# A hybrid decoder trunk: every fourth weight block's low half subtracted by GpSimd in the projection, output and query stages

## The reference

```
h = rmsnorm(x, norm1_g[l]) * (1 + sc1) + sh1
x = x + g1 * token_mixer(h, positions, w_in[l], ret_gn_g[l], sinks[l], w_out[l])
h = rmsnorm(x, norm2_g[l]) * (1 + sc2) + sh2
x = x + g2 * peer(h, peer_wq[l], k1[l], k2[l], peer_u[l], peer_v[l])
```

## Time and profile before

| | |
|---|---|
| time, median of 3 runs | 1949.06 us (1948.62 to 1949.06) |
| span of the profiled execution | 1948.0 us |
| PE busy | 1901.1 us (98%) |
| DVE busy | 1725.7 us (89%) |
| ACT busy | 1201.8 us (62%) |
| POOL busy | 575.5 us (30%) |
| `w_lo` subtractions on DVE | 664, 814.3 us, 1227 ns each |

### The profile page before, as it was taken

The page is one execution under the profiler, slowest core; times in us unless marked ns, Lnnn a source line. Parts: engine busy times, 40 slices in busy tenths (PEclk is TensorE's granted clock), DMA queues, the critical chain, the costliest instruction groups (busy, mean ns, idle before and its releaser), DMA issues.

```text
span 1948.0 us, 37761 instructions
## 1 busy us (share of the span) xinstructions
PE 1901.1 (98%) x13826; PEld 1830.6 (94%) x13826; DVE 1725.7 (89%) x3225; ACT 1201.8 (62%) x2215; POOL 575.5 (30%) x404
## 2 busy tenths in 40 slices
PE   6999999999999999999999999999999999999998
PEld 6899899999999999999978898999999999999998
DVE  7788888999799899999988978899988888999997
ACT  4478545666788645555456775466667885555554
POOL 0000000000799544555200000000019873455550
PEclk8999999999999999999999999999999999999999
DMA  9776765666565799999867756656664558999994
GB/s 338 248 254 217 261 226 176 204 204 204 203 199 191 247 377 375 370 379 373 309 225 261 251 169 221 223 187 202 205 206 164 173 173 306 373 373 366 367 381 163
DMA packets 139940, 503.72 MB, mean 259 GB/s; under 512 B 16632, under 2 KB 17272, under 8 KB 139304
## 3 DMA queue, kind: packets, MB, share of 16 engines
q1 hardware_dynamic: 115048, 411.95, 61.0%
q0 software_dynamic: 24768, 90.19, 11.8%
HBM read 496.69 MB, written 1.57 MB: 256 GB/s over the span
## 4 chain that ended last, share of the span: by engine, by line
PE 72%; DVE 20%; issue 3%; ACT 2%; DMA 2%; POOL 1%; SPq 0%; DVEq 0%; ACTq 0%
PE ps L1893 19%; PE ps L1889 12%; DVE w_lo L919 7%; PE ps L1574 7%; PE ps L1493 6%; PE ps L1489 5%; PE ps L1490 4%; PE ps L1578 4%; PE ps L1486 3%; PE ps L1849 2%; PE ps L1620 1%; DVE hot L1232 1%; DVE hot L1224 1%; ACT w_hi L596 1%; PE ps L1776 1%
## 5 line engine op out<-in xcount | busy, mean ns | idle before, releaser
L596 ACT CAST w_hi<-raw 128x1024 fp32r<-128x1024 f32 x664 | 697.1, 1050 | 687.7 <-PE ps L1889 264.4
L919 DVE TENSOR_TENSOR w_lo<-raw,w_hi 128x1024 fp32r<-128x1024 f32 x664 | 814.3, 1227 | 145.6 <-ACT w_hi L596 141.2
L571 POOL TENSOR_SCALAR hot<-con,rt 128x128 f32<-128x128 f32 x216 | 268.7, 1255 | 545.7 <-DVE neg L1404 517.0
L1574 PE MATMUL ps<-h_both,w_hi 128*128 128x432 f32 x1712 | 373.2, 359 | 0.0
L1574 PEld LDWEIGHTS ps<-h_both,w_hi 128*128 128x128 f32 x1712 | 305.6, 189 | 10.0
L1489 PE MATMUL ps<-h_both,w_hi 128*128 128x256 f32 (+1 forms) x920 | 224.3, 284 | 2.8 <-ACT big L876 2.2
L1578 PEld LDWEIGHTS ps<-h_both,w_lo 128*128 128x128 f32 x1712 | 223.4, 191 | 2.8 <-DVE w_lo L919 0.6
L1578 PE MATMUL ps<-h_both,w_lo 128*128 128x216 f32 x1712 | 224.0, 273 | 0.0
L1490 PE MATMUL ps<-h_both,w_hi 128*128 128x256 f32 (+1 forms) x920 | 220.3, 280 | 0.0
L1893 PE MATMUL ps<-p_both,w_hi 128*128 128x432 f32 x992 | 214.9, 358 | 1.4 <-DVE p_both L1329 1.4
L1893 PE MATMUL ps<-h_both,w_hi 128*128 128x432 f32 x960 | 207.8, 358 | 0.1
(11 more groups left out here) (234 smaller groups left out, 2862.2 us busy)
## 6 DMA issues: line engine op xcount, KB each, us to landing
raw<-in_u SPq DMA_DIRECT2D x256, 512.0 KB, 3.3
raw<-in_v SPq DMA_DIRECT2D x256, 512.0 KB, 6.1
raw<-in_win SPq DMA_DIRECT2D x104, 512.0 KB, 4.4
hot<-in_ada SPq DMA_DIRECT2D x62, 512.0 KB, 4.8
big<-in_ada SPq DMA_DIRECT2D x34, 512.0 KB, 6.5
raw<-in_wq SPq DMA_DIRECT2D x32, 512.0 KB, 4.6
raw<-in_wout SPq DMA_DIRECT2D x16, 512.0 KB, 4.2
big<-in_decay SPq DMA_DIRECT2D x2, 1536.0 KB, 7.9
```

Of the source, the lines that this page charges most:

```text
L571: last = nc.gpsimd.tensor_scalar(hot2[:, b % 2, t, :], iota, rt[:, 1, col], rt[:, 2, col], ALU.is_equal, ALU.mult)
L596: nc.scalar.copy(w_hi[:, j % 2, :], raw[:, j, :]).then_inc(hi_ready, 1)
L919: tt(w_lo[:, j % 2, :], raw[:, j, :], w_hi[:, j % 2, :].bitcast(F32), ALU.subtract).then_inc(lo_ready, 1)
L1574: mm(o[:, 0:2 * DENSE].rearrange("p (a t) -> p a t", a=2), w_hi[:, s, P * k:P * (k + 1)], h_both[:, :, k, 0:DENSE], start=(k == 0), stop=F ...
```

## The change

GpSimd makes the low half of some blocks, VectorE that of the others. A new table says which:

```diff
+MIX_LOWS = range(11, B_WOUT + 4), range(3, B_WOUT + 4)
+LOW_POOL = tuple(tuple(m for m in range(3, N_BLOCKS, RING) if m in MIX_LOWS[l] or B_WQ < m < B_U) for l in range(DEPTH))
+def by_pool(n):
+    return n % N_BLOCKS in LOW_POOL[n // N_BLOCKS]
+def low_count(n):
+    return sum(by_pool(k) == by_pool(n) for k in range(n + 1))
...
             def low(n, j):
+                if by_pool(n):
+                    return
                 dve.wait_ge(hi_ready, n + 1)
```

With `B_WOUT` = 52, `B_WQ` = 60, `B_U` = 76 and `RING` = 4 these are blocks 11, 15, ..., 55 of layer 0 (12 blocks), 3, 7, ..., 55 of layer 1 (14), and 63, 67, 71, 75 of either (8): 34 of 664. No block of `u` or `v` is among them. GpSimd runs, ahead of its additions of squares and behind them:

```diff
+            def low(n):
+                pool.wait_ge(hi_ready, n + 1)
+                nc.gpsimd.tensor_tensor(w_lo[:, n % 2, :], raw[:, n % RING, :], w_hi[:, n % 2, :].bitcast(F32), ALU.subtract
+                                        ).then_inc(lo_pool, 1)
...
+                lows(l, 0, B_WQ)
                 pair_squares(2 * l + 1)
+                lows(l, B_WQ, B_V)
```

Low halves are now counted by two semaphores, `lo_ready` (VectorE) and the new `lo_pool` (GpSimd). Whoever waits for one low half waits for the semaphore of its maker:

```diff
+                if n >= RING:
+                    sp.wait_ge(low_sem(n - RING), low_count(n - RING))
...
-                pe.wait_ge(lo_ready, n + 1)
+                pe.wait_ge(low_sem(n), low_count(n))
```

More of the change, by code:

```diff
@@ L341, in build @@
         raw_in = [sem(f"raw_in{s}") for s in range(RING)]
+        lo_pool = sem("lo_pool")
         hi_ready, lo_ready, block_done, out_taken = map(sem, ("hi_ready", "lo_ready", "block_done", "out_taken"))
@@ L396, in home, with low_sem @@
             return (M if m < 2 or C_AQ <= m < C_AQ + 2 else E)[m % 2]
+        def low_sem(n):
+            return lo_pool if by_pool(n) else lo_ready
         block = ctx.enter_context(nc.Block())
@@ L403, in load, with loads_between @@
                 n = base + RING * i + j
-                ge(sp, lo_ready, n - RING + 1)
+                if n >= RING:
+                    sp.wait_ge(low_sem(n - RING), low_count(n - RING))
                 sp.dma_start(raw[:, j, :], src(l, RING * i + j)).then_inc(raw_in[j], 16)
+            def loads_between(src, first, end, base, l):
+                per = [sum(by_pool(base + RING * (first - 1) + k) == by_pool(base + RING * (first - 1) + j) for k in range(RING))
+                       for j in range(RING)]
+                with sp.Fori(first, end) as i:
+                    for j in range(RING):
+                        n = base + RING * (first - 1) + j
+                        sp.wait_ge(low_sem(n), low_count(n) + per[j] * (i - first))
+                        sp.dma_start(raw[:, j, :], src(l, RING * i + j)).then_inc(raw_in[j], 16)
             ada_all = ada.rearrange("l n p d -> (l n) p d")
@@ L522, in _ @@
                     if q == 3:
-                        with sp.Fori(first, SPREAD_AT) as i:
+                        for i in (0, 1):
                             for j in range(RING):
                                 load(src, i, j, base, l)
+                        loads_between(src, 2, SPREAD_AT - 1, base, l)
+                        for j in range(RING):
+                            load(src, SPREAD_AT - 1, j, base, l)
                         sp.wait_ge(tok_copied, 2 * (l + 1))
@@ L537, in _ @@
                         first = N_U // RING
[L538 to L541, removed]
+                    assert first == count // RING
                     if q == 1:
@@ L557, in pair_squares, with lows @@
                     nc.gpsimd.tensor_tensor(sq[:, k, :], sq[:, k, :], sq[:, k + 1, :], ALU.add).then_inc(sq_paired, 1)
+            def low(n):
+                pool.wait_ge(hi_ready, n + 1)
+                nc.gpsimd.tensor_tensor(w_lo[:, n % 2, :], raw[:, n % RING, :], w_hi[:, n % 2, :].bitcast(F32), ALU.subtract
+                                        ).then_inc(lo_pool, 1)
+            def lows(l, first, end):
+                for m in LOW_POOL[l]:
+                    if first <= m < end:
+                        low(l * N_BLOCKS + m)
             for l in range(DEPTH):
@@ L577, in _ @@
                 pool.wait_ge(gate_mat, N_GATE * (l + 1))
+                used_at = [dot_at(k) for k in range(SP_STEPS)] + [mix_at(k) for k in range(SP_STEPS)]
+                low_next = B_V
                 for j in range(2 * SP_STEPS):
+                    if j >= SP_SLOTS:
+                        upto = B_V + used_at[j - SP_SLOTS] + 3
+                        lows(l, low_next, upto)
+                        low_next = max(low_next, upto)
                     if j >= SP_SLOTS:
@@ L585, in _ @@
                         bass.IndirectOffsetOnAxis(spread[:, 0, k:k + 1].bitcast(U32), 0)).then_inc(row_in[slot], 16)
+                lows(l, low_next, N_BLOCKS)
             pair_squares(2 * DEPTH)
@@ L1557, in project_pair @@
                 with_lo(0, KC - 1).then_inc(block_done, 1)
-                pe.wait_ge(lo_ready, n + 2)
+                pe.wait_ge(low_sem(n + 1), low_count(n + 1))
                 for k in range(KC):
@@ L1565, in add_half, with project_wide @@
                           skip_group_check=True)
-            def project_wide(l, m, j, after_wide=True, first=FIRST_U[0], halves=0):
+            def project_wide(l, m, j, after_wide=True, first=FIRST_U[0], halves=0, turn=0):
                 s, n = j % 2, l * N_BLOCKS + B_U + m
+                at = l * N_BLOCKS + B_U + j
                 pe.wait_ge(hi_ready, n + 1)
@@ L1575, in project_wide @@
                        start=(k == 0), stop=False, skip_group_check=True)
-                pe.wait_ge(lo_ready, n + 1)
+                per = sum(by_pool(at + k) == by_pool(at) for k in range(LONG))
+                pe.wait_ge(low_sem(at), low_count(at) + per * turn)
                 for k in range(KC):
@@ L1894, in both_y, with outputs_y, low_wait @@
                               (h_both[:, :, j - 2, 0:nd] if j >= 2 else p_both[:, j, :, 0:nd]), start=begin, stop=False, skip_group_check=True)
-                def outputs_y(i, blocks, first=False, last_ones=False):
+                def outputs_y(i, blocks, first=False, last_ones=False, turn=0):
+                    def low_wait(j):
+                        at = l * N_BLOCKS + B_V + RING * i + j
+                        per = 0
+                        if not isinstance(i, int):
+                            at = l * N_BLOCKS + B_V + RING + j
+                            per = sum(by_pool(at + k) == by_pool(at) for k in range(RING))
+                        pe.wait_ge(low_sem(at), low_count(at) + per * turn)
                     for j in range(blocks):
@@ L1908, in outputs_y @@
                                 if which == 2:
-                                    pe.wait_ge(lo_ready, n + 1)
+                                    low_wait(j)
                                 for c in range(KC):
@@ L1935, in _ @@
                 with pe.Fori(1, SP_SUM_AT // RING) as i:
-                    outputs_y(i, RING)
+                    outputs_y(i, RING, turn=i - 1)
                 sum_mixed()
```

2 lines of the change are left out of this document (1 added, 1 removed).

## The result

The changed kernel takes 1966.25 us (median of 4 runs, 1962.43 to 1966.97) against 1949.06 us: a ratio of 1.0082, 95% interval [1.0068, 1.0097]. By the medians it is 17.2 us slower. The forecast was 7.5 us slower, with a range that ended at 1964.0: the sign was right, the size was not.

What follows compares the result with a forecast made beforehand. The prediction took TensorE to set the pace. Its terms, 1.7 + 2.3 + 1.5 + 1.1 + 0.9 = 7.5 us, on the 1948.0 us span plus 1.06 us gave 1956.6 us, range 1945.5 to 1964 us.

Steps and rivals of the forecast that it cites:

- What bounds the kernel: TensorE sets the pace; VectorE costs time only where TensorE waits for it, 4.8 us in layer 0.
- Cost of one moved block: Projection, output and query stages: frees 1.14 us on VectorE, takes 2.45 us on GpSimd; the engines exclude each other.
- The four places: Tight stretches in projection and output stages of both layers: +1.7, +2.3, +1.5 and +1.1 us.
- blocks 11 to 16: Layer 0: block 11 gets 0.7 us faster, later rotations and angle instructions come late; +1.7 us.
- layer 0's output stage: Blocks 51 and 55 each delay VectorE by 1.15 us, and block 60's load hangs behind; +2.3 us.
- The other 26 moved blocks: Elsewhere, mostly free as TensorE doesn't wait for `w_lo` or VectorE reads PSUM; +0.9 us for all.
- Bookkeeping, query stages: Waits, queue order and `u` and `v` register sums cost nothing new; GpSimd isn't still at work ahead of query blocks.
- The sign of being wrong: VectorE subtractions all staying at 1.22 us, or a falling total of `w_lo` waits, would make the prediction wrong.
- rival (1): GpSimd leaves the port between its pieces and VectorE passes, so waits vanish; about 1944.5 us, chance 0.15.
- (2): Collisions fall mostly into VectorE's idle time, gains and losses cancel within 3 us; 1946 to 1952.5 us, chance 0.25.
- (3): Behind gapless VectorE work moved blocks take 4 to 5 us, 15 of 34 hold TensorE up; about 1966 us, chance 0.12.

Runs made afterwards that it cites:

- Relief alone: Changed kernel without GpSimd's 34 subtractions, nobody making these low halves, so its result is wrong; 1947.89 us, -1.9 us against the kernel before.
- the kernel with the ends: Changed kernel with only 16 projection and output stage blocks moved to GpSimd; 1956.63 us, +6.4 us against the kernel before.
- the ten attention blocks alone: Changed kernel with only blocks 27, 31, 35, 39 and 43 of each layer on GpSimd; 1958.44 us, +8.0 us against the kernel before.
- the kernel with the empty table: Changed kernel with no block moved, VectorE making all 664 low halves and the bookkeeping kept; 1950.86 us, ratio 1.000 against the kernel before.
- pieces: Changed kernel with each moved GpSimd subtraction cut into four of 256 columns; 1969.89 us, +17.9 us against the kernel before.
- A GpSimd copy with one input: VectorE makes every low half; GpSimd runs copies of 1024 columns into an idle buffer at 26 points; 1955.16 us, +4.9 us against the kernel before.
- the subtraction over 512: VectorE makes every low half; GpSimd runs 26 dummy subtractions over 512 columns; 1955.44 us, +5.7 us against the kernel before.
- two blocks: Changed kernel with only block 39 of layer 0 and block 27 of layer 1 on GpSimd; 1956.03 us, +6.6 us against the kernel before.
- the long dummy: VectorE makes every low half; GpSimd runs 26 dummy subtractions over 1024 columns into an idle buffer; 1965.26 us, +14.4 us against the kernel before.
- the eight: Changed kernel with only attention blocks 27, 31, 35, 43 of layer 0 and 31, 35, 39, 43 of layer 1 moved; 1953.01 us, +3.1 us.

## Why the prediction was wrong, point by point

- **What bounds the kernel**: held. Relief alone is worth 2 us, less than the 4.8 us of waits that the forecast read in layer 0.
- **Cost of one moved block**: held. 2.38 us against 2.45; full exclusion; VectorE stands still for up to 2.2 us (two-column addition: 0.16 to 2.36 us), 1.5 us on average, for 1.14 us freed. The Trainium skill (SBUF — State Buffer, "SBUF: two separate sides") calls the shared pair "an exclusive lock, not a bandwidth split", held for the whole instruction, against VectorE instructions with two SBUF inputs or in a two-port mode. The trace agrees for the lock (four masked maxima that read PSUM, beside GpSimd's 2.39 us from 147.38, take their usual 0.48 us; the first of them is shown):

```profile
147.38 2.39 POOL L591 TENSOR_TENSOR w_lo<-raw,w_hi 128x1024 fp32r<-128x1024 f32 x1 [14.03 <-ACT w_hi L646]
147.70 0.48 DVE L1142 CUSTOM_DVE_ANT_0 big<-ps,big,vec 128x256 f32<-128x256 f32 x1 [0.72 <-PE ps L1763]
```

- **The four places** (forecast 6.6 us): 7.15 us by the shifts, 6.4 us by the kernel with the ends. The working of single places was rougher than the sum. In blocks 11 to 16, block 11 went as written (the second rotation stood until 63.1), but at block 15 what stood still was a cast ahead of the angle instructions, which the forecast had not named:

```profile
73.42 3.12 POOL L591 TENSOR_TENSOR w_lo<-raw,w_hi 128x1024 fp32r<-128x1024 f32 x1 [10.90 <-ACT w_hi L646]
74.22 2.47 DVE L994 CAST iota<-con 128x256 f16<-128x256 f32 x1
```

  In layer 0's output stage, GpSimd's subtraction of block 55 holds up the conditioning product at 227.95, TensorE waits 2.19 us, and block 60's load follows the low half of block 56 as forecast (a timeline, and the chain's row for the load):

```profile
227.95 3.43 DVE L978 CUSTOM_DVE_ANT_0 hot<-hot,cond 128x1024 f32<-128x1024 f32 x1
236.10 1.01 PEld L1830 LDWEIGHTS ps<-h_both,w_lo 128*128 128x128 f32 x8 [2.19 <-DVE w_lo L971]
```
```profile
236.07 7.92 DMA raw<-in_wq
```

- **"The other 26 moved blocks ... I take +0.9 us"**: this step failed; 9.85 us by the shifts, +8.0 us [5.3, 10.7] for the ten attention blocks alone. "TensorE doesn't wait for `w_lo` at all" was true there and beside the point. I had checked one of VectorE's results, the low half, for slack. In attention VectorE also makes the norm terms, the masked scores and the probabilities, and TensorE and ScalarE take these in fixed order with less slack than 2.3 us. The earlier trace rows showed that already: in attention the longest waits were for L1110, not for `w_lo`. I spread 1.2 us of lateness over a few blocks instead of looking up what stands behind each moved block on VectorE.
- **The clock** wasn't in the sum. The earlier trace rows showed 1.00, and I took that as given; the change made two waits over 2 us, and 1.5 us was lost behind each.
- **Bookkeeping, query stages**: held, at nothing, each to within some 2 us. The 0.01 us per block that the forecast gave as the most a register sum could cost stands in no row; the kernel with the empty table has all these sums.
- **The sign of being wrong** was badly chosen. The forecast named VectorE subtractions that all stay at 1.22 us, as a sign against itself and for rival (1). They do stay there beside the 34 holds (1.72 us at most over the run, as before), and the collisions are real all the same: they fell on rotations (2.89 us), conditioning products (3.43 us) and short additions.
- **Rivals.** (1), relief without collision: out, since VectorE is held and relief is 2 us, not 4.8. (2), cancelling: out. (3), GpSimd starving, came near in its number (1966) but its mechanism isn't there: no subtraction took over 3.4 us, and TensorE's waits name no low half of GpSimd. It took pieces to make it so.

In short: the mechanism of the collision was right; the term for the 26 other blocks was too small by 9 us, because it looked at `w_lo` alone, and 3 of the 9 us are the clock's, which had no term. That the sign came out does not rest on that term.

## What to carry to other kernels

A second engine that shares a port isn't free because its instruction stream is. Price the hold as lateness of the whole saturated engine, and then go through every result that stands behind the hold in its order, however short its instruction, with the slack of each taker; the result that was moved is only one of them. Ask of each new wait near 2 us whether TensorE's clock falls behind it.

## What the runs showed of the hardware

- The lock goes by instruction: a VectorE addition over 2 columns is held up as long (2.21 us for 0.16) as a product over 1024 (3.42 us for 1.22). A GpSimd copy with one input locks VectorE out like a subtraction; what counts is its length (1.04 us and +4.9 us, against 1.04 us and +5.7 us for the subtraction over 512).
- On VectorE's side one-input instructions are held too: the cast of 256 columns took 2.47 us instead of 0.28. Whether it ran in a two-port mode, as the rule above would want, no run tells.
- GpSimd's two-input subtraction takes 0.72 us for 256 columns and 2.38 us for 1024; cut in four it would need 4 x 0.72 = 2.9 us undisturbed (an estimate), and took 3.7 beside VectorE. When both want the port they take turns, instruction by instruction.
- A wait of TensorE of 2.0 to 2.5 us was followed by a fall to the lower clock in some cases and not in others: after 2.53 and 2.22 us in the changed kernel yes, after 2.19 us (at 236.10) no; with ten blocks after 2.52 us yes and 2.37 no; with two blocks after 2.52 us no and 2.39 yes; beside the long dummy after 2.03 us (at 169.62) yes and after 2.04 (at 65.30) no. A fall costs 1.5 us. So the same edit can differ by 3 us between executions and places that wait equally long, and what decides it stays open.
- Block 31 of layer 0 cost 1.4 us in the full change and nothing with the eight or the ten, and half a microsecond of timing makes the difference. In the change GpSimd's subtraction begins at 130.97, just ahead of the last norm-term addition (L1133, at 131.13), which then takes 2.27 us instead of 0.17; the masked maxima stand behind it and TensorE waits 1.53 us. With the ten it begins at 128.99, just behind that addition (128.66), and holds up a conditioning product (2.62 us instead of 1.22), and TensorE has no such wait behind it.
